# A two-block transformer kernel: relative-position bias rows made on TensorE for every partition instead of by a DRAM broadcast

## The reference

```python
# first block, attention part (cut)
h = rms_norm(x, norm1_g)
proj = h @ w_in                                    # 1024 x 3072
q_d, k_d, v_d, q_m, k_m, v_m = jnp.split(proj, splits, axis=-1)
q, k = rms_norm(q, q_g), rms_norm(k, k_g)          # per head of 64, for both kinds of attention
logits = einsum(q, k) * 64 ** -0.5
dist = query_position - key_position
bias = bias_table[t5_bucket(dist)]                 # 32 buckets x 12 heads
logits = where(dist >= 0, logits + bias, -1e30)
p = softmax(logits)                                # 4 differential heads (two maps each), 8 plain heads
x = x + concat(y_d, y_m) @ w_out
x = x + mixture_of_experts(rms_norm(x))            # 32 experts, 2 per token
# second block: FFN, sliding attention and mLSTM side by side, FFN, final norm
```

## Time and profile before

| what | value |
|---|---|
| median of 3 runs | 1157.88 us |
| the profiled execution, its own time | 1157.88 us |
| its span | 1156.1 us |
| PE busy | 1080.9 us, 93% of the span |
| DVE busy | 567.8 us, 49% |
| ACT busy | 413.8 us, 36% |
| POOL busy | 45.6 us, 4% |
| mean transfer rate | 207 GB/s |

### The profile page before, as it was taken

One profiled execution on the slowest core, in us unless ns is written; L12 is line 12 of the kernel. 1 busy time (PEld: TensorE's weight loads), 2 busy tenths in 40 slices (PEclk: granted clock), 3 DMA queues, 4 the chain that ended last, 5 costly groups with the idle time before them and its releaser, 6 DMA issues.

```text
span 1156.1 us, 13710 instructions
## 1 busy us (share of the span) xinstructions
PE 1080.9 (93%) x5547; PEld 821.6 (71%) x5547; DVE 567.8 (49%) x712; ACT 413.8 (36%) x518; POOL 45.6 (4%) x56
## 2 busy tenths in 40 slices
PE   7697899999999999999999999967899999999996
PEld 6585787444444447888887998846688887888885
DVE  4456734222222226445444547488756654444453
ACT  3345422111111114333334445364344334343332
POOL 2311000000000000000000000010000000000000
PEclk9897999999999999999999999877899999999999
DMA  7953048979999966555555355421055544655540
GB/s 224 330 180 145 1 180 331 417 321 401 405 419 402 413 252 206 175 189 181 181 182 181 129 183 177 140 83 37 1 201 183 203 158 137 203 171 183 195 146 36
DMA packets 101838, 239.51 MB, mean 207 GB/s; under 512 B 11690, under 2 KB 56834, under 8 KB 86306
## 3 DMA queue, kind: packets, MB, share of 16 engines
q1 hardware_dynamic: 99874, 229.05, 55.1%
q0 software_dynamic: 1920, 9.85, 2.5%
HBM read 237.81 MB, written 3.43 MB: 209 GB/s over the span
## 4 chain that ended last, share of the span: by engine, by line
PE 85%; DVE 8%; ACT 3%; DMA 2%; issue 2%; POOL 1%; POOLq 0%; DVEq 0%; ACTq 0%
PE banks L920 19%; PE banks L922 19%; PE banks L921 19%; PE banks L1123 10%; PE banks L1138 5%; PE banks L1113 3%; PE banks L1104 3%; PE banks L927 2%; DMA bias_rows<-bias_row 1%; PE banks L1238 1%; PE banks L1005 1%; PE banks L1052 1%; DVE token_major L1453 1%; PE banks L939 1%; DVE head_stats L1923 1%
## 5 line engine op out<-in xcount | busy, mean ns | idle before, releaser
L1473 DVE TENSOR_TENSOR weights_lo<-raw_weights,weights_hi 128x2048 fp32r<-128x2048 f32 x116 | 265.6, 2291 | 237.7 <-ACT weights_hi L612 237.7
L612 ACT ACTIVATE weights_hi<-raw_weights 128x2048 fp32r<-128x2048 f32 x116 | 221.6, 1912 | 210.9 <-PE banks L922 183.8
L920 PE MATMUL banks<-weights_hi,normed_T_hi 128*128 128x512 f32 (+1 forms) x624 | 248.2, 398 | 5.0 <-DVE stage L1789 3.1
L922 PE MATMUL banks<-weights_hi,normed_T_lo 128*128 128x512 f32 (+1 forms) x624 | 243.5, 390 | 0.0
L921 PE MATMUL banks<-weights_lo,normed_T_hi 128*128 128x512 f32 (+1 forms) x624 | 243.1, 390 | 0.0
L920 PEld LDWEIGHTS banks<-weights_hi,normed_T_hi 128*128 128x128 f32 x624 | 118.7, 190 | 36.8 <-issue 10.1
L922 PEld LDWEIGHTS banks<-weights_hi,normed_T_lo 128*128 128x128 f32 x624 | 118.2, 189 | 24.9
L921 PEld LDWEIGHTS banks<-weights_lo,normed_T_hi 128*128 128x128 f32 x624 | 118.5, 190 | 22.7
L1123 PE MATMUL banks<-expert_weights,stage 128*64 128x512 f32 x256 | 113.2, 595 | 0.0
L920 PE MATMUL banks<-weights_hi,ffn_hidden_T_hi 128*128 128x512 f32 x176 | 68.7, 390 | 3.0 <-DVE ffn_hidden_T_lo L1793 3.0
L922 PE MATMUL banks<-weights_hi,ffn_hidden_T_lo 128*128 128x512 f32 x176 | 68.5, 389 | 0.0
(11 more groups left out here) (306 smaller groups left out, 1571.0 us busy)
## 6 DMA issues: line engine op xcount, KB each, us to landing
raw_weights<-in_w_in SPq DMA_DIRECT2D x38, 1024.0 KB, 5.1
raw_weights<-in_ffn_w_gate SPq DMA_DIRECT2D x44, 512.0 KB, 3.9
raw_weights<-in_ffn_w_up SPq DMA_DIRECT2D x44, 512.0 KB, 4.9
raw_weights<-in_ffn_w_down SPq DMA_DIRECT2D x22, 1024.0 KB, 4.8
expert_weights<-in_w_gate SPq DMA_DIRECT2D x16, 1024.0 KB, 7.3
expert_weights<-in_w_up SPq DMA_DIRECT2D x16, 1024.0 KB, 9.4
expert_weights<-in_w_down SPq DMA_DIRECT2D x16, 1024.0 KB, 9.5
stage<-in_w_down SPq DMA_DIRECT2D x9, 1024.0 KB, 11.3
```

The lines of the kernel that those rows point to most:

```text
L612: ins = eng.activation(w_hi[:, slot, :], raw, ACT.Copy)
L920: eng.matmul(dst, x[0], w[0], start=first_one, stop=False)
L922: return eng.matmul(dst, x[1], w[0], start=False, stop=last_one)
L1473: ins = eng.tensor_tensor(w_lo[:, slot, :], raw, w_hi[:, slot, :], ALU.subtract)
```

## The change

There are five edits.

1. The 33x12 table is widened on DVE to 33x12x128, the same value 128 times (`relb`). PE multiplies each head's 33x128 slice by the one-hot matrix, which gives that head's row on all 128 partitions: 12 products with 384 columns, into banks 6 and 7 in turn. DVE copies each (128x384). They stand after block 6 on PE and after `take_projection(2)` on DVE.
2. POOL stores the 128x12x384 result to DRAM in one transfer and reads it back skewed; the broadcast is gone.
3. POOL's first four roots of heads stand ahead of the store; the store, its wait, the read back and the gain load stand between the fourth and the fifth.
4. `head_squares_of` is gone: each tile's sum, scale, root and multiplication are in one row in `take_projection`, after the split, on one shared set of statistics.
5. The transpose of the small vectors stands ahead of the last `stay_warm`, before block 0, and DVE takes its result before the splits of pieces 1 and 2.

```diff
-        bias_row = nc.dram_tensor("bias_row", [N_BIAS, DIST_COLS], F32, kind="Internal").ap()
-        bias_rows = nc.dram_tensor("bias_rows", [P, N_BIAS * DIST_COLS], F32, kind="Internal").ap()
+        bias_rows = nc.dram_tensor("bias_rows", [N_BIAS, P, DIST_COLS], F32, kind="Internal").ap()
...
@@ POOL
-            eng.wait_ge(bias_copied, 1)
-            eng.dma_start(bias_row, bias_stage).then_inc(bias_stored, 16)
+            for _ in range(2 * TILES):
+                root(hs[:, 0, 1, 0:8])
+            eng.wait_ge(bias_copied, N_BIAS)
+            eng.dma_start(bias_rows.rearrange("h p m -> p h m"), bias_stage).then_inc(bias_stored, 16)
             eng.wait_ge(bias_stored, 16)
-            eng.dma_start(bias_rows, bias_row.rearrange("h m -> (h m)").partition_broadcast(P)).then_inc(bias_stored, 16)
-            eng.wait_ge(bias_stored, 32)
...
             eng.dma_start(bias, skewed).then_inc(bias_loaded, 16)
             eng.wait_ge(normed, TILES * (N1 + 1))
             load_gain("norm2_g")
-            for _ in range(4):
-                for t in range(TILES):
-                    root(hs[:, t, 1, 0:8])
+            for _ in range(2 * TILES):
+                root(hs[:, 0, 1, 0:8])
@@ PE
             transpose8(T_N1, tok, lambda t: (normed, TILES * N1 + t + 1), True, (12, 4))
+            eng.wait_ge(vec_loaded, 16 * N_VEC)
+            eng.transpose(PS[:, 3, 0:V_ROWS], vec_rows[:, :], ident[0:V_ROWS, 0:V_ROWS]).then_inc(vec_T, 1)
             stay_warm(14, 2)
...
-                    if kh == 0 and c == 0:
-                        small_tables()
+                    if kh == 0 and c == 3:
+
+                        eng.wait_ge(rel_wide, 1)
+                        for h in range(N_BIAS):
+                            if h >= 2:
+                                eng.wait_ge(bias_copied, h - 1)
+                            eng.matmul(PS[:, 6 + h % 2, 0:DIST_COLS], relb[:, h, :], onehot[:, :], start=True, stop=True
+                                       ).then_inc(bias_ps, 1)
@@ DVE
+            feed(0)
+            eng.wait_ge(rel_loaded, 32)
+            eng.tensor_copy(relb[:, :, :], wide(relx[:, :], P)).then_inc(rel_wide, 1)
...
-                    eng.wait_ge(root_out, roots[0] - 1 + t)
+                    eng.wait_ge(proj_sq, n + 1)
+                    eng.tensor_reduce(hs[:, 0, 0, 0:8], tok[:, t, HALF:].rearrange("p (h d) -> p h d", d=HEAD),
+                                      AX_X, ALU.add).then_inc(proj_sq_read, 1)
+                    eng.wait_ge(proj_sq_read, n + 1)
+                    rsqrt(hs[:, 0, 1, 0:8], hs[:, 0, 0, 0:8], HEAD)
...
             for c in range(6):
-                if c:
-                    head_squares_of(c - 1)
                 feed(2 * c)
                 if c:
                     take_projection(c - 1)
+                if c == 3:
+                    for h in range(N_BIAS):
+                        eng.wait_ge(bias_ps, h + 1)
+                        eng.tensor_copy(bias_stage[:, h, :], PS[:, 6 + h % 2, 0:DIST_COLS]).then_inc(bias_copied, 1)
```

More of the change, by code:

```diff
@@ L175, in two_blocks @@
         bias = view(6144, N_BIAS, SEQ)
-        bias_stage = LP[0:N_BIAS, 0:DIST_COLS]
-        onehot = LP[0:BUCKETS + 1, DIST_COLS:2 * DIST_COLS]
-        lam_rows = LP[:, 2 * DIST_COLS:2 * DIST_COLS + 4 * HEAD].rearrange("p (n d) -> p n d", n=4)
+        bias_stage = LP[:, 0:N_BIAS * DIST_COLS].rearrange("p (h m) -> p h m", h=N_BIAS)
+        BS = N_BIAS * DIST_COLS
+        relb = LP[0:BUCKETS + 1, BS:BS + N_BIAS * P].rearrange("p (h q) -> p h q", h=N_BIAS)
+        onehot = LP[0:BUCKETS + 1, BS + N_BIAS * P:BS + N_BIAS * P + DIST_COLS]
+        lam_rows = LP[:, BS + N_BIAS * P + DIST_COLS:BS + N_BIAS * P + DIST_COLS + 4 * HEAD].rearrange("p (n d) -> p n d", n=4)
         xgT = LP[:, 0:KT * RING * SLOTS].rearrange("p (k s) -> p k s", k=KT)
@@ L243, in two_blocks @@
         consts, root_in, root_out = sem("consts"), sem("root_in"), sem("root_out")
-        vec_T, vec_ready = sem("vec_T"), sem("vec_ready")
+        vec_T, vec_ready, rel_wide = sem("vec_T"), sem("vec_ready"), sem("rel_wide")
         bias_ps, bias_copied = sem("bias_ps"), sem("bias_copied")
@@ L533, in _ @@
             norm_root(N1)
-            eng.wait_ge(bias_copied, 1)
-            eng.dma_start(bias_row, bias_stage).then_inc(bias_stored, 16)
+            for _ in range(2 * TILES):
+                root(hs[:, 0, 1, 0:8])
+            eng.wait_ge(bias_copied, N_BIAS)
+            eng.dma_start(bias_rows.rearrange("h p m -> p h m"), bias_stage).then_inc(bias_stored, 16)
             eng.wait_ge(bias_stored, 16)
-            eng.dma_start(bias_rows, bias_row.rearrange("h m -> (h m)").partition_broadcast(P)).then_inc(bias_stored, 16)
-            eng.wait_ge(bias_stored, 32)
             skewed = bass.AP(tensor=bias_rows.tensor, offset=P - 1,
-                             ap=[[N_BIAS * DIST_COLS - 1, P], [DIST_COLS, N_BIAS], [1, SEQ]])
+                             ap=[[DIST_COLS - 1, P], [P * DIST_COLS, N_BIAS], [1, SEQ]])
             eng.dma_start(bias, skewed).then_inc(bias_loaded, 16)
@@ L1513, in _ @@
             t8_split(T_N1, hT)
-            feed(0)
             eng.wait_ge(vec_T, 1)
@@ L1520, in _ @@
                               ALU.mult).then_inc(vec_ready, 1)
-            eng.wait_ge(bias_ps, 1)
-            eng.tensor_copy(bias_stage, PS[0:N_BIAS, 2, 0:DIST_COLS]).then_inc(bias_copied, 1)
+            feed(0)
+            eng.wait_ge(rel_loaded, 32)
+            eng.tensor_copy(relb[:, :, :], wide(relx[:, :], P)).then_inc(rel_wide, 1)
             eng.wait_ge(lam_loaded, 64)
@@ L1530, in _ @@
             n_qk = [0]
[L1532 to L1543, removed]
             def take_projection(c):
@@ L1556, in take_projection @@
                     eng.tensor_tensor(tok[:, t, 0:HALF].rearrange("p (h d) -> p h d", d=HEAD),
-                                      bank.rearrange("p (h d) -> p h d", d=HEAD), wide(hs[:, t, 1, 0:8], HEAD),
+                                      bank.rearrange("p (h d) -> p h d", d=HEAD), wide(hs[:, 0, 1, 0:8], HEAD),
                                       ALU.mult).then_inc(proj_used, 1)
```

## The result

The changed kernel takes 1166.62 us (median; 1163.68 to 1169.72), against 1156.01 us for the kernel before, timed beside it. The ratio is 1.0099 with a 95% interval of 1.0079 to 1.0119: about 11 us slower, 9 to 14 with the interval. The prediction said 1162.5, with a range of 1157.5 to 1166.5. The sign was right and the size was not: the sum had 4.6 us above the kernel before, and 10.6 were measured. The time lies only 0.1 us outside the range because the kernel before ran at 1156.01 beside it and not at the 1157.88 that the prediction started from; that closeness is luck.

What follows compares the result with a forecast made beforehand. PE was taken to set the pace, stalled at group 0 by POOL's order. Stall -8.6 and twelve products +8.6 cancelled by block 7; POOL's hold and the last pair left +4.6 on 1157.88: 1162.5 us, range 1157.5 to 1166.5.

Steps and rivals of the forecast that it cites:

- Where PE stands still before, and why: Before group 0's transposes: PE idles 8.62 us for POOL's order of work, clock falls to half; removing it gives -8.6.
- The head, +3.9 and hidden: Kernel start: small vectors there by 17.4, block 0 begins at 20.8, not 16.86, hidden while DVE is later.
- rival (c): Head: small vectors come late or the warm-up runs at half clock; together 1164 to 1165 us; chance 0.08.
- the step on group 0: Serial units on DVE end at 40.3 and 43.75; block 4 begins at 44.3 at full clock instead of 51.11.
- The twelve products, +8.6: After block 6 on PE: twelve products at 0.72 us each, with nothing to hide them.
- The store of 11.6 us and POOL's hold: Group 3: store lands at 82.95, POOL free at 84.85, 3.1 late; block 10 at 91.25, +3.7.
- The last pair and the end: After group 3's units: group 4's units end at 103.15, masked logits at 108.85 against 104.27, +4.6 in all.
- (a): Store quick, 8.4 us or less, POOL free in time: +1.3, 1159.2 us; chance 0.27.
- (b): Store of 13 to 15 us or PE's clock falling in its idle from 86.5 to 91: 1165 to 1167; chance 0.12.
- (d): Faster: the twelve products do not cost PE what they take, the end near +0.5; chance 0.08.

Runs made afterwards that it cites:

- run 7: The kernel before with only POOL's order changed, four roots ahead of the wait for the broadcast; ratio 0.9903, median 1145.18 us.
- Run 1: The changed kernel with the transpose of the small vectors put back behind block 0; ratio 1.0085 to the kernel before.
- run 4: The changed kernel with the vector transpose back behind block 0 and the twelve products zero-padded to 128 rows; ratio 1.0067 to the kernel before, median 1163.62 us.
- run 2: The changed kernel with both operands of the twelve products zero-padded from 33 to 128 rows; ratio 1.0076 to the kernel before.
- run 3: The changed kernel with the twelve products in four banks in turn instead of two, still 33 rows; ratio 1.0091 to the kernel before.
- run 10: Run 7's kernel plus the twelve products on 33 rows, vector transpose behind block 0, two roots beside the store; ratio 1.0043 to the kernel before, median 1161.45 us.
- run 5: The changed kernel with vector transpose behind block 0, products on 128 rows, and two POOL roots between the store's issue and its wait; ratio 1.0044 to the kernel before.
- run 9: Run 7's kernel plus the twelve products on 128 rows, vector transpose behind block 0, two roots beside the store; ratio 0.9975 to the kernel before, median 1154.43 us.

## Why the prediction was wrong

**Where PE stands still before, and why.** Right. The stall was POOL's order, 8.6 us with its slow clock, and the order alone gives 12.1 at the logits (run 7). I costed it as what the change could win, and the serial units and the later stalls kept part of it from showing: with sums ahead of the split block 4 begins at 40.77, with serial units at 43.5.

**The head, +3.9 and hidden.** Wrong, and the first step that failed. The vectors landed at 19.14, not by 17.4. The bound rested on a lambda row that was issued later and had landed at 17.4, on the condition that the queue keeps its order. It does not. In the changed kernel itself the lambda row issued at 13.12 landed at 17.5, ahead of the vectors, whose last transfer was issued at 12.06:

```profile
stage<-in_lambda_q SPq DMA_DIRECT2D x1, 32.0 KB, 4.4
```

Why the vectors took longer is not shown; 19 small transfers had to be complete. And the wait was not costed with the clock, except as rival (c), to which I gave 0.08: full speed was assumed for the warm-up behind the pause, which became 5.2 us. Block 0 came 7.9 late, and DVE's later units hid only half of it: block 4 began at 48.33, against 44.3 predicted. Run 1, which takes this away, brings block 4 to 44.25 and run 4 to 43.84. So the step on group 0 was right, on a wrong start. (Its terms add up to 3.51 us a unit and not to the 3.45 written; measured, a unit follows the one before it after 3.3.)

**The twelve products, +8.6.** The step that failed most: 13.66 us, and 1.5 more in block 7. Of this the pitch at full clock was mis-sized a little (0.77 in run 2 against 0.72; a wait for a copy also holds up the next weight load). The rest, 4.5 us, and block 7's slow start are the clock, and neither the sum nor a rival had it. I took it that a busy PE keeps its clock, as the fall of the earlier trace rows had followed a pause. The trace of before could have told me otherwise. In the second block PE runs 48 products with 16 columns (on all 128 rows) back to back from 727.71 on, behind full-size products and without a pause, and the clock falls at about 730.6 all the same (windows of PE alone):

```profile
728.00:730.00 2.00, 2.00 (x20) 1.00 0.92 294
730.00:731.00 1.00, 1.00 (x10) 0.82 0.83 289
731.00:732.00 1.00, 1.00 (x7) 0.50 1.04 408
```

**The store of 11.6 us and POOL's hold.** The store landed 10.4 us after its issue in every run that has it, 0.6 below the 11.0 to 12.1 of the sum and above the 8.4 at which it begins to count. The rule of the Trainium skill that I weighed there ("DMA: Bandwidth & Descriptors", "Anatomy of one DMA — SWDGE (gpsimd) path") gives an estimate of 7.4 us, too low by 3 for this store with weight loads beside it. The hold of 3.1 showed as 1.8 in run 4, and as 0.35 in the changed kernel. There the slow clock delayed block 7 together with the store, and the demand came later (scale at 92.30, root at 92.95).

**The last pair and the end.** From the end of block 7 to the logits I had 33.3 us and the trace has 29.9, mainly by the smaller hold. All together at the logits: +4.3 from the head, +5.1 from the twelve, +1.5 in block 7, -3.4 behind it, which is the 7.5 between 108.85 and 116.33.

**Rivals.** (a) is out, the store is not quick. (b) named a slow clock, but in the wrong place; (c) was the right mechanism with the right cause and half the result; (d) had nothing for it. The range took in each mishap alone, and the case was two together, one of them not on the list.

## What to carry over

When an engine that serves small requests also waits for transfers, put the requests ahead of the wait: moving four roots gave 1% here, and rebuilding the data path to avoid the wait lost 1%. Cost a block of small float32 products not by their columns alone but by what they do to the granted clock, for themselves and for what follows; here, filling the rows with zeros kept it and cost nothing on PE (the median record is 0.48 us with 33 rows and 0.49 with 128). A wait on PE put ahead of a warm-up undoes the warm-up, and when a group of transfers lands should be bounded by its own last landing, not by a neighbour's.

## What the runs showed of the hardware

- With 33 of 128 rows in use and PE busy without a break, the granted clock went from full to half within the twelve products in every execution profiled (the changed kernel, runs 1, 3 and 10); the same twelve on 128 rows, in four runs (2, 4, 5 and 9), kept it at full. Between run 9 and run 10, and between the changed kernel and run 2, only the rows in use differ, but for the clearing on DVE at the start that fills them.
- Products on few rows are not the only ones that do this. Products with 16 columns on all 128 rows, back to back, brought the clock from full to half at about 730.6 us in the kernel before (rows above). What the two have in common, these runs do not tell.
- Around a pause of 2.65 us on PE the clock fell in two executions (runs 1 and 5) and did not in one (run 4). Such a fall cost 2.8 us in run 1 and 1.6 in run 5.
- A later stretch, the same in all these kernels, varies too. Between the mix norm's second root and the gated gain on POOL, the kernel before needs 122.4 us, the changed one 120.8, run 9 122.4 and run 10 119.2. It holds the products with 16 columns, and behind them the clock stands at half for 10.2, 6.8, 10.2 and 3.4 us, which accounts for the differences (3.4 us more at half clock cost 1.7). The profiled spans of runs 9 and 10 are equal (1154.6), though their logits are 4.75 apart and their medians 7. So the span of one profiled execution is not a verdict on a change in one stage.
